# Normalising each head's probabilities before they are turned, and making the first branch's gate with channels on the partitions

## The reference

```python
def dsa_attention(q, k, v, qi, ki, wi, k_sel):
    ...
        logits = jnp.einsum('bthd,btjhd->bthj', q_b.astype(jnp.float32),
                            k_g.astype(jnp.float32)) * (Dh ** -0.5)
        logits = jnp.where(valid[:, :, None, :], logits, -jnp.inf)
        p = jax.nn.softmax(logits, axis=-1)
        out = jnp.einsum('bthj,btjhd->bthd', p, v_g.astype(jnp.float32))
...
        y_a = (o_a * jax.nn.silu(a_z)) @ w_branch_a[l]
...
        y_b = (h_b * jax.nn.silu(b_z)) @ w_branch_b[l]
        merged = jax.nn.sigmoid(g_a) * y_a + jax.nn.sigmoid(g_b) * y_b
        x = x + merged @ w_out[l]
```

## Time and profile before

| | |
|---|---|
| median of 3 runs | 505.14 us (505.14 to 505.3) |
| profiled execution | 505.35 us |
| its span in the trace | 503.6 us |
| PE busy | 494.5 us, 98% |
| DVE, ACT, POOL busy | 261.4, 239.2, 213.0 us |
| granted TensorE clock | 0.998 of full |
| attention, first logits to last turning | about 234 to 310 us of the span |
| units az | about 301 to 323 us |

### The profile page before, as it was taken

One profiled execution on the slowest core, in us unless ns is written; L12 is line 12 of the kernel. 1 busy time (PEld: TensorE's weight loads), 2 busy tenths in 40 slices (PEclk: granted clock), 3 DMA queues, 4 the chain that ended last, 5 costly groups with the idle time before them and its releaser, 6 DMA issues.

```text
span 503.6 us, 6823 instructions
## 1 busy us (share of the span) xinstructions
PE 494.5 (98%) x2518; PEld 411.6 (82%) x2518; DVE 261.4 (52%) x575; ACT 239.2 (47%) x434; POOL 213.0 (42%) x130
## 2 busy tenths in 40 slices
PE   8999999999999999999999999999999999999995
PEld 7688888888888888888788888888888888887885
DVE  3865777877899936525655567531111011125433
ACT  6757655555554455536568652413330333152322
POOL 0675131333344444247487451246534663373000
PEclk9999999999999999999999999999999999999999
DMA  8654432212343243112223112043234426453111
GB/s 284 188 153 128 126 87 79 84 48 80 83 111 99 85 117 104 52 43 85 57 70 85 43 43 65 20 125 104 62 87 125 126 58 193 126 149 144 42 55 72
DMA packets 44841, 48.94 MB, mean 97 GB/s; under 512 B 4996, under 2 KB 30212, under 8 KB 44808
## 3 DMA queue, kind: packets, MB, share of 16 engines
q1 hardware_dynamic: 43944, 47.65, 32.3%
q10 hardware_dynamic: 864, 0.86, 0.5%
HBM read 46.40 MB, written 2.11 MB: 96 GB/s over the span
## 4 chain that ended last, share of the span: by engine, by line
PE 94%; DMA 2%; SPq 1%; POOL 1%; ACT 1%; DVE 1%; issue 1%; DVEq 0%
PE pj L1486 24%; PE pj L1487 24%; PE pj L1488 24%; DMA w_raw<-in_w_in 2%; PE ob L1617 2%; PE tr L1606 2%; PE qb L1554 2%; PE qb L1553 2%; PE ob L1487 1%; PE qb L1487 1%; PE ob L1488 1%; PE qb L1488 1%; PE ob L1486 1%; PE qb L1486 1%; PE tr L1541 1%; PE qb L1601 1%
## 5 line engine op out<-in xcount | busy, mean ns | idle before, releaser
L529 POOL TENSOR_TENSOR w_lo<-w_raw,w_hi 128x1024 fp32r<-128x1024 f32 x70 | 168.9, 2424 | 156.3 <-ACT w_hi L875 156.0
L1486 PE MATMUL pj<-w_hi,h_hi 128*128 128x512 f32 x272 | 109.6, 403 | 0.0
L1488 PE MATMUL pj<-w_hi,h_lo 128*128 128x512 f32 x272 | 106.5, 392 | 0.0
L1487 PE MATMUL pj<-w_lo,h_hi 128*128 128x512 f32 x272 | 106.4, 391 | 0.0
L1486 PE MATMUL pj<-h_hi,w_hi 128*128 128x512 f32 (+1 forms) x200 | 78.1, 390 | 1.0 <-DVE h_lo L1129 1.0
L875 ACT ACTIVATE w_hi<-w_raw 128x1024 fp32r<-128x1024 f32 (+1 forms) x72 | 73.5, 1045 | 9.8 <-DMA w_raw<-in_w_out 6.3
L1488 PE MATMUL pj<-h_hi,w_lo 128*128 128x512 f32 (+1 forms) x200 | 77.9, 389 | 0.0
L1487 PE MATMUL pj<-h_lo,w_hi 128*128 128x512 f32 (+1 forms) x200 | 77.8, 389 | 0.0
L1488 PEld LDWEIGHTS pj<-w_hi,h_lo 128*128 128x128 f32 x272 | 51.1, 188 | 11.4
L1486 PEld LDWEIGHTS pj<-w_hi,h_hi 128*128 128x128 f32 x272 | 51.2, 188 | 8.3 <-issue 0.2
L1487 PEld LDWEIGHTS pj<-w_lo,h_hi 128*128 128x128 f32 x272 | 51.3, 188 | 8.0
(11 more groups left out here) (216 smaller groups left out, 817.3 us busy)
## 6 DMA issues: line engine op xcount, KB each, us to landing
w_raw<-in_w_in SPq DMA_DIRECT2D x60, 512.0 KB, 3.6
w_raw<-in_w_out SPq DMA_DIRECT2D x5, 512.0 KB, 3.5
x_tok<-in_x SPq DMA_DIRECT2D x4, 512.0 KB, 5.3
w_raw<-in_w_branch_a SPq DMA_DIRECT2D x8, 256.0 KB, 2.9
w_raw<-in_w_branch_b SPq DMA_DIRECT2D x8, 256.0 KB, 3.3
x_again<-in_x SPq DMA_DIRECT2D x1, 2048.0 KB, 9.3
w_late<-in_w_out SPq DMA_DIRECT2D x3, 512.0 KB, 6.1
out<-y_norm SPq DMA_DIRECT2D x4, 320.0 KB, 2.3
```

The costliest lines, as they stand in the source:

```text
L529: eng.tensor_tensor(lo[:, 0:m], raw_slot(n)[:, 0:m], hi[:, 0:m].bitcast(F32), ALU.subtract).then_inc(lo_by_dve if n in DVE_SLOTS else lo_b ...
L1486: pe.matmul(bank, a_hi, b_hi, start=first, stop=False)
L1487: pe.matmul(bank, a_hi, b_lo, start=False, stop=False)
L1488: return pe.matmul(bank, a_lo, b_hi, start=False, stop=last)
```

## The change

- In the units az the operands are exchanged: the weights' tile of 128 channels is loaded and `h` moves, so the unit comes out with channels on the partitions (unit number b is a tile of channels now). Its gate goes to the new tile `gate_a`.
- The jobs `out_a_chan` are gone: PE no longer turns the gate.
- In front of the turning of each head, a new DVE job `scale_a` takes the reciprocal of the head's sum and multiplies the head's `probs` by it in place. It stands first at the place behind the head's logits. PE's turning waits for it (`probs_scaled`).
- `gate_a` multiplies gate and output by channel tile on DVE, `rest_a` makes `oa_hi` and `oa_lo` on ACT and DVE. They hang at the last quarters of az and, for the last tiles, behind it (`LAST_SIDE`).

```diff
         q = attn_place(p)
+        if 1 <= p <= len(ATTN):
+            put(q, "scale_a", p - 1)
...
-        if j < TILES - 1:
-            put(first["az"] + 4 * j + 6, "out_a_chan", j)
+    put(first["az"] + 12, "gate_a", 0)
+    put(first["az"] + 13, "gate_a", 1)
+    put(first["az"] + 14, "rest_a", 0)
+    put(first["az"] + 15, "gate_a", 2)
+    put(first["az"] + 15, "rest_a", 1)
...
-OA_LO_AT = {first_quarter("az") + 4 * j + 8: j for j in range(TILES - 2)}
-LAST_SIDE = ("out_a_chan", TILES - 1)
+LAST_SIDE = (("gate_a", 3), ("rest_a", 2), ("rest_a", 3))
...
+        gate_a = at("gate_a", [P, KW, SEQ], F32, z_e)
...
-                    wait_full(sp, LAST_SIDE)
+                    wait_full(sp, LAST_PV)
+                    sp.wait_ge(zt_made, 2 * TILES)
...
+                elif kind == "rest_a":
+                    b = job[1]
+                    act.wait_ge(oa_gated, b + 1)
+                    act.activation(oa_hi[:, b, :].rearrange("p (i t) -> p i t", t=P), o_at[:, :, b, :], ACT.Copy)\
+                        .then_inc(o_hi, 1)
...
+                if c == 0:
+                    for job in LAST_SIDE:
+                        job_side(job)
...
-                        act.wait_ge(o_lo, TILES + 2)
+                        act.wait_ge(o_lo, 2 * TILES)
...
-                    if c == 1 and s == 0:
-                        act.wait_ge(o_lo, 2 * TILES)
...
-                        s = i * A_HEADS
-                        dve.wait_ge(probs_made, s + A_HEADS)
-                        link(dve.reciprocal(p_rec[:, s:s + A_HEADS], p_sum[:, s:s + A_HEADS]))
...
+                elif kind == "scale_a":
+                    s = job[1]
+                    w = (ATTN[s][0] + 1) * P
+                    dve.wait_ge(probs_made, s + 1)
+                    link(dve.reciprocal(p_rec[:, s:s + 1], p_sum[:, s:s + 1]))
+                    dve.tensor_scalar(probs[:, s % 2, 0:w], probs[:, s % 2, 0:w], p_rec[:, s:s + 1], None, ALU.mult)\
+                        .then_inc(probs_scaled, 1)
+                elif kind == "gate_a":
+                    b = job[1]
+                    dve.wait_ge(zt_made, TILES + b + 1)
+                    dve.wait_ge(o_at_made, TILES)
+                    gate = gate_a[:, (b + 2) % KW, :].rearrange("p (i t) -> p i t", t=P)
+                    dve.scalar_tensor_tensor(out=o_at[:, :, b, :], in0=gate, scalar=0.5, in1=o_at[:, :, b, :],
+                                             op0=ALU.mult, op1=ALU.mult).then_inc(oa_gated, 1)
+                elif kind == "rest_a":
+                    b = job[1]
+                    dve.wait_ge(oa_gated, b + 1)
+                    dve.wait_ge(o_hi, TILES + b + 1)
+                    oa = oa_lo[:, b, :].rearrange("p (i t) -> p i t", t=P)
+                    dve.tensor_tensor(oa, o_at[:, :, b, :],
+                                      oa_hi[:, b, :].rearrange("p (i t) -> p i t", t=P).bitcast(F32), ALU.subtract)\
+                        .then_inc(o_lo, 1)
...
+                    if g == "bz" and j >= 2:
+                        wait_full(dve, ("out_b_chan", j - 2))
+                    if g == "az" and j >= 2:
...
+                        dve.wait_ge(q_lo_made, 2 * TILES)
+                        dve.wait_ge(q_doubled, 2 * TILES)
...
                                                    in1=pj[u % 2][:, :], op0=ALU.add, op1=ALU.mult)
...
-                elif g == "az":
-                    ring = gated[:, (TILES + j) % 2, :]
-                    dve.wait_ge(zt_made, TILES + j + 1)
-                    heads = ring.rearrange("p (h d) -> p h d", d=A_DIM)
-                    rec = p_rec[:, j * A_HEADS:(j + 1) * A_HEADS]
-                    dve.tensor_tensor(heads, heads, rec.unsqueeze(2).to_broadcast([P, A_HEADS, A_DIM]), ALU.mult)\
...
-                    pe.wait_ge(probs_made, s + 1)
+                    pe.wait_ge(probs_scaled, s + 1)
...
-                        if g in CHAN_GROUPS:
+                        if g in CHAN_GROUPS + ("az",):
                             a, b = w_part(n, c + j * P, c + (j + 1) * P), h_part(k, 0, SEQ)
```

More of the change, by code:

```diff
@@ L178, in fills @@
     bank, before, order = {}, {}, {}
-    for job in [job for p in sorted(SIDE) for job in SIDE[p] if job[0] not in NOT_PE] + [LAST_SIDE]:
+    for job in [job for p in sorted(SIDE) for job in SIDE[p] if job[0] not in NOT_PE]:
         order[job] = len(order)
@@ L193 @@
 BANK, BEFORE, ORDER = fills()
-OUT_ORDER = sorted([("out_a_chan", j) for j in range(TILES)] + [("out_b_chan", j) for j in range(TILES)],
-                   key=ORDER.get)
+LAST_PV = ("pv_a", len(ATTN) // QUAD - 1)
 ROUNDS = TOPK // 8
@@ L968, in job_side @@
                         .then_inc(probs_made, 1)
-                elif kind in ("out_a_chan", "out_b_chan"):
-                    j = job[1]
[L971 to L978, removed]
+                elif kind == "rest_a":
[3 more added lines that the diff above has]
+                        .then_inc(o_hi, 1)
+                elif kind == "out_b_chan":
+                    j = job[1]
+                    wait_full(act, job)
+                    act.activation(ob_hi[:, :, j * P:(j + 1) * P],
+                                   bank_of(job)[:, :].rearrange("p (b t) -> p b t", t=P), ACT.Copy, scale=0.5)\
+                        .then_inc(o_hi, 1)
             def evacuate(u):
@@ L1327, in job_side @@
                     j = job[1]
                     src = bank_of(job)[:, :].rearrange("p (b t) -> p b t", t=P)
[L1329 to L1334, removed]
-                        dve.wait_ge(o_hi, OUT_ORDER.index(job) + 1)
-                        dve.scalar_tensor_tensor(
-                            out=ob_lo[:, :, j * P:(j + 1) * P], in0=src, scalar=0.5,
-                            in1=ob_hi[:, :, j * P:(j + 1) * P].bitcast(F32), op0=ALU.mult, op1=ALU.subtract)\
-                            .then_inc(o_lo, 1)
@@ L1341, in oa_remainder @@
[L1341 to L1346 removed]
+                    dve.wait_ge(o_hi, j + 1)
+                    dve.scalar_tensor_tensor(
+                        out=ob_lo[:, :, j * P:(j + 1) * P], in0=src, scalar=0.5,
+                        in1=ob_hi[:, :, j * P:(j + 1) * P].bitcast(F32), op0=ALU.mult, op1=ALU.subtract)\
+                        .then_inc(o_lo, 1)
@@ L1619, in side @@
                                                 tile_position=(0, e * A_DIM))
-                elif kind in ("out_a_chan", "out_b_chan"):
-                    pe.wait_ge(gated_a_made if kind == "out_a_chan" else gated_b_made, job[1] + 1)
-                    ring = gated[:, OUT_ORDER.index(job) % 2, :]
+                elif kind == "out_b_chan":
+                    pe.wait_ge(gated_b_made, job[1] + 1)
+                    ring = gated[:, job[1] % 2, :]
                     for b in range(KW):
@@ L1669, in _ @@
                     ins.then_inc(unit_full, 1)
-                    if c == 0 and s == 0:
-                        side(LAST_SIDE)
                 n = GATE0 + 3 * c + 2
```

31 lines of the change are left out of this document (8 added, 23 removed).

## The result

The changed kernel takes 526.37 us (median of 4 runs, 525.72 to 528.54) against 505.14: a ratio of 1.0427, with a 95% interval of 1.0396 to 1.0457. The forecast was 521.9 with a range of 508.5 to 531.5.

The account below looks back on a forecast made before the run. PE was taken to bound the kernel, without reserve. From the profiled 505.35 us: 1.7 less for the gate, 8.2 more for term A, 10.3 for term B, 522.15; as median 521.9, range 508.5 to 531.5.

Parts of the forecast that it names:

- the closed cycle: Attention, per head on DVE and ACT: masked logits, exponential, reciprocal and scale, copy; 2.79 us at 512 columns against PE's 2.28.
- the lock: Attention: DVE's scale stands until a running GpSimd (POOL) instruction ends; 10.3 us more, bounds 0 and 18.
- The gate: PE in the attention: four turnings of the gate go, 0.43 us each, 1.7 us less.
- term A: Attention: PE's loss to DVE's longer cycle, 6.7 us for heads 12 to 27 plus 1.5 for 0 to 11: 8.2.
- term B: Attention: 14.6 of 32 scales wait for POOL, 13.7 us, three quarters counted: 10.3 us, bounds 0 and 18.
- Every new wait of PE is a loss in full: PE in the attention: it sets the time without reserve, having waited 0.2 us from 232 to 345 us.
- The tail: Last products of gate and output, in front of the first sigmoid: 0 us, bounds 0 and 1.
- no collision: Rival, attention: the scale does not collide with POOL, term B is 0; 511.6 us (508 to 515), chance 0.28.
- DVE's idle time takes it all: Rival, attention: DVE's idle time absorbs the scale, only the 1.7 us gain is left; 503.4 us, chance 0.09.
- Both errors cancel near zero: Rival, attention: a cycle of about 2.4 us and no collisions; 505 us, chance 0.03.
- What was to be seen: Attention: PE waits some 18 us for `probs` or `probs_t`; scale median near 0.45, tail 1 to 2.7 us; fewer transposes.

Follow-up runs that it names:

- the gate alone: Changed kernel without `scale_a`, so the division by the head's sum is left out and the turning waits for the exponential: 503.68 us, ratio 0.997 against the kernel before.
- the form that does not lock: Changed kernel, same order, with DVE's scale multiplication also writing a row sum that nothing reads: 517.37 us, ratio 1.0242 against the kernel before.

## Why the prediction was right

The mechanism held: the closed cycle and the lock are both there, and together they make most of the loss. The time missed by 4.5 us, 0.9%. The sizes are less good than that: one term was too high and one too low by about 4 us each, which cancels by luck, and the clock was missing.

- **The gate**: 1.7 us less forecast, 1.5 measured.
- **The cycle** (term A): 2.79 us forecast at 512 columns and 2.78 measured, 2.35 and 2.34 at 384. From the product of heads 8 to 11, at 264.88, to that of heads 24 to 27, at 322.94, the changed kernel takes 58.1 us. PE's own pace is 41.0, stretched scales in it are 9.7, which leaves 7.4 for the cycle and the slower matmuls at 277.91 and 292.07. These are 2.8 (1.5 + 1.3 by the comparison above), so if each stretched scale counts in full, the cycle is 4.6; forecast 6.7.
- **The lock** (term B): 13.7 us in 14.6 instructions forecast, 14.5 in 12 measured. I then counted three quarters of it, 10.3, for slack in the first eight heads. That factor was wrong. The product of heads 8 to 11 came at 264.88 instead of 259.95, 4.9 us later, and the scales up to there were stretched by just 4.9. The slack of some 0.3 us a head is no use against a wait of 2.2. The 1.5 us of term A for those heads were not there. So term B was 4.9 + 9.7 = 14.6 where 10.3 stood, term A 4.6 where 8.2 stood: 19.2 against 18.5.
- **The clock**: the step that was missing. "Every new wait of PE is a loss in full" is too little: the matmuls behind three of the waits ran at a reduced clock, and the sum had priced all of them at their old durations. From the product at 322.94 to the next six matmuls behind the third turning it is 332.66 - 322.94 = 9.7 us, in the run with 8 extra matmuls 328.29 - 321.41 = 6.9: 2.8 us in one place. With the 2.8 of the other two it is 5.6 in the profiled execution, and the parts close: 19.2 + 5.6 = 24.8 of the 25.0 between its 528.5 and the 503.5 of the gate alone. In the median the clock costs about 3.3 us, the larger part of the miss; 0.7 are the two terms, 0.2 the gate.
- **The tail**: 0 forecast. With the gate alone nothing is lost there; with the whole change I read no wait of PE at it.

Of the rivals, "no collision" falls with the stretched scales, and "DVE's idle time takes it all" with 21 waits for ACT. The number of the first, 511.6, was not tested as it stands: the form that does not lock gives 517.4, but it is 7.8 us more work for DVE, and one product still ran at the lower clock. "Both errors cancel near zero" needed a cycle of 2.4 at 512 columns, which is 2.78.

What was to be seen came: 17.8 us of PE's waits where 18 were named (19.9 in full), put down to `probs` and `probs_t`; a median of the scale of 0.49 with a tail to 2.45; 16 transposes fewer on PE in all. Only the distance behind POOL was smaller, 0.09 to 0.29 us where 0.3 to 0.5 were named.

## What to carry to other kernels

Before an instruction is put into an in-order engine, look for the cycle that it closes: the engine's busy share (52% here) says nothing, the sum from its wait back to itself does. An instruction that may be locked out by GpSimd is to be priced at the rest of GpSimd's instruction, in full, wherever a step behind it has less slack than that. And where a change gives TensorE new waits as long as those here, 2.3 to 3.8 us, the matmuls behind them may come at a lower clock and take up to twice as long: leave room for it in the range. The waits of a view are to be checked against the spacing of starts before they are added up.

## What the runs showed of the hardware

- The plain float32 scale of one SBUF tile runs 512 columns in 0.49 us and stood in 12 of 32 cases, for up to 2.2 us, until POOL had finished; the form with a row sum takes 0.75 us and 0.08 for its read, and never stood in 96 instances of three kernels, of which 17 to 19 in each ran beside a large instruction of POOL.
- TensorE's clock fell behind waits of 2.32 us (in the run with the row sum, where the product took 3.49 us instead of 1.97), 2.50, 2.73 and 3.78, but not behind one of 2.74, nor of 2.04 (in the run with the row sum). It fell to near half, 0.52 of full in the worst 4 us. The changed kernel's four executions had mean clocks of 0.984 to 0.995, and the one with the lowest was the longest.
- Eight extra matmuls in front of each of four waits kept the clock whole (0.999) and made the kernel 1.9 us faster.
